# Nine landing buffers through the expert stage, experts taken in pairs, with table loads and projections placed elsewhere

## The reference: what is computed

```python
x = x + jnp.concatenate([fox_out, rwkv_out], axis=-1) @ w_out[i]   # fox_out has a factor sigmoid(fog)
x = x + moe_ffn(rmsnorm(x, moe_norm[i]), w_router[i], b_router[i], w_gu[i], b_gu[i],
                w_down[i], b_down[i])
gate = jax.nn.sigmoid(rmsnorm(x, ple_norm[i]) @ w_ple_gate[i])
x = x + gate * (p[i] @ w_ple_proj[i])
return rmsnorm(x, final_norm)
# an expert: hh = xb @ w_gu[e] + b_gu[e]; glu = min(hh[:, :FF], 7); lin = clip(hh[:, FF:], -7, 7)
#            y = (glu * sigmoid(1.702 * glu) * (lin + 1)) @ w_down[e] + b_down[e]
```

## Time and profile before

| | |
|---|---|
| time, median of 3 runs | 1285.59 us |
| time of the profiled execution | 1289.38 us |
| its span, first to last instruction | 1287.6 us |
| TensorE busy / weight loads | 1191.3 us (93%) / 522.4 us |
| VectorE, ScalarE busy | 307.5 us (24%), 181.1 us (14%) |
| DMA | 434.97 MB, mean 338 GB/s; 428 to 429 GB/s in most slices of the second half |
| chain that ended last | DMA 46%, PE 46%, DVE 4%, ACT 2% |
| granted TensorE clock, mean | 0.971 |

### The profile page before, as it was taken

How to read it: one execution, slowest core, us unless ns; L and a number is a source line. 1 busy time by engine, 2 the same in 40 slices (tenths; PEclk the granted TensorE clock), 3 DMA queues, 4 the chain that set the end, 5 groups by cost and what they waited for, 6 DMA issues and landing times.

```text
span 1287.6 us, 16763 instructions
## 1 busy us (share of the span) xinstructions
PE 1191.3 (93%) x6900; PEld 522.4 (41%) x6900; DVE 307.5 (24%) x631; ACT 181.1 (14%) x331; POOL 0.2 (0%) x4
## 2 busy tenths in 40 slices
PE   6999996899999999999999999999999999999994
PEld 5888765654333333333333323233333233223333
DVE  2444533333121212111111112111112111111136
ACT  2411422133000000000000000000100000000022
POOL 0000000000000000000000000000000000000000
PEclk9999996698999999999999999999999999999997
DMA  9631020165969999999999999999999999999940
GB/s 385 263 132 67 23 87 26 39 240 220 394 281 427 429 429 428 429 429 428 429 429 428 429 428 429 429 428 429 429 429 428 429 429 429 428 429 429 429 183 33
DMA packets 31793, 434.97 MB, mean 338 GB/s; under 512 B 3921, under 2 KB 4049, under 8 KB 5265
## 3 DMA queue, kind: packets, MB, share of 16 engines
q1 hardware_dynamic: 31760, 434.50, 80.3%
HBM read 433.44 MB, written 1.05 MB: 337 GB/s over the span
## 4 chain that ended last, share of the span: by engine, by line
DMA 46%; PE 46%; DVE 4%; ACT 2%; issue 1%; SPq 0%; DVEq 0%; ACTq 0%
DMA ring<-in_we 46%; PE PS L785 21%; PE PS L450 7%; PE PS L492 3%; PE PS L634 2%; PE PS L587 1%; PE PS L745 1%; PE PS L760 1%; PE PS L863 1%; DVE ring L1517 1%; PE PS L462 1%; PE PS L455 1%; PE PS L799 1%; PE PS L686 1%; PE PS L564 1%
## 5 line engine op out<-in xcount | busy, mean ns | idle before, releaser
L785 PE MATMUL PS<-ring,FV 128*64 128x512 f32 x3024 | 680.6, 597 | 42.6 <-DMA ring<-in_we 41.9
L785 PEld LDWEIGHTS PS<-ring,FV 128*64 128x64 f32 x3024 | 207.4, 137 | 483.1 <-issue 392.5
L450 PE MATMUL PS<-hT,ring 128*128 128x256 f32 x416 | 95.0, 387 | 0.8 <-ACT hT L917 0.8
L450 PEld LDWEIGHTS PS<-hT,ring 128*128 128x128 f32 x416 | 79.5, 193 | 13.1 <-ACT hT L917 1.2
L1387 DVE TENSOR_SCALAR rz<-con,lora 64x64 f32<-64x64 f32 x30 | 7.4, 246 | 303.6 <-PE PS L785 303.6
L1466 DVE TENSOR_SCALAR hT<-PS 128x512 f32<-128x512 f32 x32 | 22.1, 691 | 197.6 <-PE PS L785 197.6
L1144 DVE TENSOR_TENSOR FV<-PS,prm 128x512 f32<-128x512 f32 x32 | 22.1, 691 | 184.7 <-PE PS L752 184.7
L1071 ACT ACTIVATE FV<-PS 128x512 f32<-128x512 f32 x32 | 19.1, 597 | 310.1 <-PE PS L826 310.1
L745 PE MATMUL PS<-xq,rz 128*64 128x512 f32 x256 | 62.0, 605 | 0.0
L760 PE MATMUL PS<-B,rz 64*128 64x512 f32 x248 | 61.6, 615 | 0.0
L1069 ACT ACTIVATE hT<-hT 128x512 f32<-128x512 f32 x32 | 20.1, 630 | 267.0 <-DVE hT L1458 267.0
(11 more groups left out here) (255 smaller groups left out, 736.2 us busy)
## 6 DMA issues: line engine op xcount, KB each, us to landing
ring<-in_we SPq DMA_DIRECT2D x189, 2048.0 KB, 23.1
ring<-in_wz SPq DMA_DIRECT2D x7, 2048.0 KB, 21.6
B<-in_we SPq DMA_DIRECT2D x3, 2048.0 KB, 7.7
ring<-in_wo SPq DMA_DIRECT2D x2, 2048.0 KB, 7.9
ring<-in_wgate SPq DMA_DIRECT2D x2, 2048.0 KB, 24.3
con<-in_con SPq DMA_DIRECT2D x1, 1181.0 KB, 7.2
xq<-in_x SPq DMA_DIRECT2D x2, 512.0 KB, 4.6
ring<-in_wz SPq DMA_DIRECT2D x1, 1024.0 KB, 9.4
```

Source lines behind the costliest of these rows:

```text
L450: mm = pe.matmul(bank(n % 4, SEQ), w[:, k, at:at + P], hT[:, k, :], **flags)
L785: mm = pe.matmul(PS[64 * h:64 * h + 64, bank_, :], lhs(4 * (q % 2) + k), w[:, k, h, :], start=(first and k == 0), stop=(q % 2 == 1 and k = ...
```

## The change

1. **Landing buffers.** The three `extra` buffers are kept for the whole expert stage. Pieces 0 to 2 of every item land in `ring[0..2]`; pieces 3 to 5 land in `ring[3..5]` for even items and in `extra` for odd ones. SP issues pieces 3 to 5 of item i+1 behind pieces 0 to 2 of item i, when item i-1 has used its own pieces 3 to 5. Only at the end is the order 0 to 5 for the last item.
2. **Pairs.** All engines' places in the buffers must be known in the program, so TensorE's and SP's loops take two items in a turn: items 0 and 1, then 14 turns, then the last two items written out. The number of items is rounded up to an even one.
3. **Projection.** The second half of `w_ple_proj` lands in `LZ` and `lora` during item 1 (two transfers of 256 KB); its products (`project_late`) run in the last item and behind the last scatter, and stay in PSUM. In routing only the first halves are computed, and the ranks of the first token block stand ahead of them.
4. **Sigmoid of the attention gate.** Instead of four Sigmoids among the `z` steps: four copies, and one Tanh over all 1024 columns (step `fg`) behind `ffl`; sigmoid(x) = (1 + tanh(x/2)) / 2, with the half in the values `FV`.
5. **Table loads in routing.** The set with both Ln and Exp is loaded before `var`; the copy `T11` stands ahead of the second `rms`.
6. **Tail.** The gate is ScalarE's Sigmoid, so `L1516` and `L1517` go; two table loads are added; the last chunk has a PSUM bank of its own, so its product does not wait for the chunk before; the last scaling is split over both engines, and four stores of 256 KB replace one of 512 KB and two of 256 KB. Gate weights land in slots 3 and 4, free since item 30.

```diff
+        wgate = ring[:, 3:5, :]
+        gfin = ring[:, 5, 0:D]
+        wproj1 = LZ[:, :, :].rearrange("p a b -> p (a b)"), lora[:, 0:PW]
...
+            def place(q, odd):
+                return extra[q - 3] if odd and q >= 3 else ring[:, q, :]
...
+            for q in range(6):
                 sp.wait_ge(s_used, q + 1)
-                expert_piece(1, q)
+                sp.dma_start(place(q, q < 3), t["we"][1 if q < 3 else 2, q]).then_inc(landed(q, q < 3), 16)
+            sp.wait_ge(s_used, 7)
+            for k in range(2):
+                sp.dma_start(wproj1[k], t["wproj"][1, :, k * PW:(k + 1) * PW]).then_inc(s_ple1, 16)
...
+            def stage(i, odd, qs=range(6)):
+                e = [sp.value_load(EI[0:1, bass.ds(i + a, 1)], min_val=0, max_val=NE - 1) for a in range(1 + (len(qs) > 3))]
+                for q in qs:
+                    sp.wait_ge(s_used, 6 * i + (q - 5))
+                    sp.dma_start(place(q, odd == (q < 3)), t["we"][bass.ds(e[q // 3], 1), q, :, :].rearrange("a p n -> (a p) n"))\
+                        .then_inc(landed(q, odd == (q < 3)), 16)
+            with sp.Fori(0, pairs) as p:
+                stage(2 * p + 2, False)
+                stage(2 * p + 3, True)
+            stage(2 * last_pair, False, range(3))
+            stage(2 * last_pair + 1, True, range(3))
...
+            with pe.Fori(0, pairs) as p:
+                item(2 * p + 2, False)
+                item(2 * p + 3, True)
+            item(2 * last_pair, False)
+            last_item = 2 * last_pair + 1
+            item(last_item, True, last=True)
...
+                if last:
+                    pe.wait_ge(s_ple1, 32)
+                    project_late(0)
                 pe.wait_ge(s_eact, i + 1)
...
             scatter_last()
+            project_late(1)
...
-            pe.wait_ge(s_tact, tact_at["gate3"])
             finish(gates(1, 1, range(KD), 256, 512), "tpe", "gate4")
...
-                    fin(act.activation(FG[:, n - 22, :], bank(n % 4, SEQ), ACT.Sigmoid), f"z{n}")
+                    fin(act.activation(FG[:, n - 22, :], bank(n % 4, SEQ), ACT.Copy), f"z{n}")
...
+                        act.preload_act_table_set("exp_and_others")
+                        act.wait_ge(s_act, act_at[f"z{NZ - 1}"])
+                        fin(act.activation(FG[:, :, :], FG[:, :, :], ACT.Tanh, scale=0.5), "fg")
...
+            act.preload_act_table_set("natural_log_exp_and_others")
             pe_done("var")
...
+            turned(1, 1)
             rms(1)
-            turned(1, 1)
...
+            act.preload_act_table_set("sigmoid_and_others")
+            act.wait_ge(s_tact, tact_at["rstd1"])
+            gated(0, 0, 0, 512, 0, 0)
...
-                fin_t(v.tensor_scalar(sig, sig, 1.0, None, ALU.add), f"one{g}")
-                fin_t(v.reciprocal(sig, sig), f"inv{g}")
-                fin_t(tt(sig, PP[:, b, c0:c1], sig, ALU.mult), f"gp{g}")
+                v.wait_ge(s_tpe, tpe_at["pl1"])
+                fin_t(tt(sig, p, sig, ALU.mult), f"gp{g}")
                 fin_t(tt(xs[:, b, c0:c1], xs[:, b, c0:c1], sig, ALU.add), f"x4{g}")
```

More of the change, by code:

```diff
@@ L412, in _ @@
+            sp.wait_ge(s_tdve, tdve_at["out11"])
+            store(1, 1)
+            sp.wait_ge(s_tact, tact_at["out01"])
+            store(0, 1)
+            sp.wait_ge(s_tdve, tdve_at["out00"])
+            store(0, 0)
+            sp.wait_ge(s_out, 16 * 4)
         @block.tensor
@@ L770, in scatter_last, with product @@
                     finish(mm, "tpe", f"s{b}")
[L772 to L782 removed]
+            def product(i, odd, q, bank_, lhs, first):
+                weights = extra[q - 3] if odd and q >= 3 else ring[:, q, :]
+                w = weights.rearrange("p (k h c) -> p k h c", k=4, h=2)
+                if q < 3:
+                    pe.wait_ge(s_we[q], 16 * i + 16)
+                elif odd:
+                    pe.wait_ge(s_odd[q - 3], 8 * i + 8)
+                else:
+                    pe.wait_ge(s_we[q], 8 * i + 16)
                 for k in range(4):
@@ L792, in _, with item @@
             x_of, act_of = half_of(xT), half_of(aT)
-            def item(i, first=False, last=False):
+            def item(i, odd, first=False, last=False):
                 pe.wait_ge(s_ohb, i + 1)
@@ L1106, in _, with root @@
-            CHUNKS = ((0, 0, 512), (0, 512, 1024), (1, 0, 512), (1, 512, 768), (1, 768, 1024))
-            for g, (b, c0, c1) in enumerate(CHUNKS):
-                q = c0 // PW
+                    square(f"sq{b}{q}", 2 * b + q, xs[:, b, q * PW:(q + 1) * PW], PW * (2 * b + q))
+            def root(name, dst, ss, bias):
+                fin_t(act.activation(dst, ss, ACT.Ln, bias=bias, scale=1.0 / D), f"ln{name}")
+                act.wait_ge(s_tact, tact_at[f"ln{name}"])
+                fin_t(act.activation(dst, dst, ACT.Exp, scale=-0.5), f"rstd{name}")
@@ L1120, in _ @@
-            act.wait_ge(s_tdve, tdve_at["fin2"])
-            act.wait_ge(s_tact, tact_at["root1"])
-            fin_t(act.activation(xs[:, 1, 0:PW], xs[:, 1, 0:PW], ACT.Copy, scale=col[:, 15:16]), "out2")
+                square(f"sq{g}", 20 + g, xs[:, b, c0:c1], 4 * PW + (PW * g if g < 3 else 3 * PW))
+            transposed(0)
+            act.preload_act_table_set("natural_log_exp_and_others")
+            act.wait_ge(s_tdve, tdve_at["half0"])
+            act.wait_ge(s_tact, tact_at["sq01"])
@@ L1606 @@
             "brt": rep(a["b_router"]), "gfin": rep(a["final_norm"]),
-            "pT": chunks(a["p"][0, 0].T), "wproj": chunks(a["w_ple_proj"][0]),
+            "pT": chunks(a["p"][0, 0].T), "wproj": np.stack([chunks(a["w_ple_proj"][0][:, q * PW:(q + 1) * PW]) for q in range(2)]),
             "wo": np.stack([chunks(a["w_out"][0][:, q * PW:(q + 1) * PW]) for q in range(2)]),
```

243 lines of the change are left out of this document (122 added, 121 removed).

## The result

In one comparison the changed kernel took 1281.45 us (median of 6 runs, 1277.59 to 1284.25) and the kernel before 1288.03 us (6 runs, 1284.89 to 1289.76). The ratio is 0.9948, 95% interval 0.9925 to 0.9972: faster by 6.6 us, about half of the 13.5 us that were forecast, and 1.45 us above the forecast range. Two later comparisons gave the same: 7.2 and 7.9 us. The base matters too: the forecast took its gain off 1285.59 us, the median of the first 3 of those 6 runs; in the four comparisons the kernel before had medians of 1288.0, 1288.4, 1287.1 and 1285.7 us.

The account below looks back on a forecast made before the run. It took the expert stage to be bound by TensorE up to about 540 us, then by a full DMA queue. Terms +3.8 - 7.2 + 0.2 - 10.3 = -13.5 off 1285.6 gave 1272 us, range 1263 to 1280.

Parts of the forecast that it names:

- routing: Stage from `var` to item 0: earlier copies, ranks ahead of the projection and half its weights give -7.2 us, bounds -3.5 and -8.
- experts: Expert stage: the filled hole's 11.3 us lead is spent on the longer way behind the last wait, +0.2 us.
- tail: End of the kernel: gate products run without a stop and TensorE bounds the chunks, -10.3 us, bounds -7 and -12.
- mixing: Ahead of `q5`: table load and Tanh on the path +2.3, clock 1.5, sum +3.8 us, bounds +2.3 to +5.7.
- allowance of 1.5 us: Mixing: added for a possible fall to half clock after TensorE stands idle for 2.5 us.
- the lead counts in full: Rival: DMA alone decides the experts' end, so 11.3 us come on top, 1261 us; chance 0.08.
- the third term: Expert stage: the late half of the projection's weights delays the landing of item 30's piece 2 by 1.2 us.
- The work behind the last wait: Expert stage: TensorE's work from item 30's piece 2 to the stage's end, counted as 46.2 us.
- its four passes cost 1.7 at full clock: Routing: the halved first projection was to take 1.7 us once its weights landed at 295.8.
- one of the bounds (-3.5): Routing's smaller gain, if the clock stays at half through the ranks or the weights land as late as before.
- routing meets its transfer: Rival: projection weights land as before and the clock stays low, 3.7 us lost, 1276 us; chance 0.10.
- The jump: Rival: TensorE's doubled loop stalls at its jump back; at 8 us a turn 49 us, 1321 us; chance 0.06.

Follow-up runs that it names:

- E1: The changed kernel again with no edit, compared with the kernel before: median 1281.21 us, ratio 0.9928.
- E3: The changed kernel with the attention gate as before, four Sigmoids among the z steps and no Tanh: median 1277.16 us, ratio 0.9907 to the kernel before.
- E9: The kernel before with only mixing's edit, plain gate copies and one Tanh with its table load ahead of `q5`: median 1290.1 us, ratio 1.0034.
- E11: The changed kernel once more as it is, beside a run with mixing as before: 1277.77 us, ratio 0.9937 to the kernel before.
- E10: The changed kernel with the mixing stage as before, measured a second time: 1274.5 us, ratio 0.9911 to the kernel before.
- E2: The changed kernel with the weight stream back in the order 0 to 5 of each item from item 19 on: median 1265.53 us, ratio 0.9819.
- E5: The kernel before with only the nine buffers, paired loops and new order of the weight stream: median 1287.38 us, ratio 0.9996.
- E4: The changed kernel with the late half of the projection's weights issued ahead of the last item's pieces 0 to 2, not in item 1: median 1275.53 us, ratio 0.9906.
- E8: The changed kernel with natural stream order from item 19, the attention gate as before and late projection weights issued near the end: median 1264.31 us, ratio 0.9824.
- E6: The changed kernel with the tail's gate again as Exp, addition and reciprocal, the last chunk keeping its own bank: median 1286.70 us, ratio 1.0011.
- E7: The kernel before with only routing's table load moved ahead of `var` and `T11` copied ahead of the second `rms`: median 1287.00 us, ratio 0.9995.

## Why the prediction was half right

Measured terms: routing, experts and tail from the profiles (three executions of the kernel before's form of a stage, nine of the changed routing, six of the changed expert stage), mixing from the medians.

| term, us | forecast | measured | from |
|---|---|---|---|
| mixing | +3.8 | +3.9 | E1 less E3 4.05, E9 4.4, E11 less E10 3.3 |
| routing | -7.2 | -5.0 | 51.4, 51.9, 52.5 against 44.7 to 48.1, mean 46.9 |
| experts | +0.2 | +2.5 | 925.5 three times, against 927.3 to 928.7, mean 928.0 |
| tail | -10.3 | -9.6 | 52.2 to 52.3, against 42.6 |
| sum | -13.5 | -8.2 | medians: -6.6, -7.2, -7.9 |

**Mixing** was right, in its mechanism (the wait for `q5`, 2.56 us) and in its size. The allowance of 1.5 us for a clock that "need not happen" to fall was sound too: the clock fell right behind the wait in four of seven executions, at up to 1.6 us each (E9), about 0.9 in the mean. The remaining half microsecond can't be told from the spread: the granted clock later in this stage differs so much between executions of one program (mixing 258.3, 258.7 and 267.65 us) that no single pair tells.

**Experts.** The main claim held: the hole was filled, the last wait moved to piece 2 of item 30, the loop did not stall, and the lead was spent by three more pieces ahead of the last wait. E2 shows it, by giving 12.4 us of the stage back with nothing but another order; "the lead counts in full" falls for the changed kernel's order. The sizes of these two terms held as well: E5 has the new order and the filled hole but not the projection's transfers, and there the piece is used 3.7 us later than in before, where 14.7 - 11.3 = 3.4 was counted.

The step that failed is the third term, "the late half of the projection's weights, 0.5 MB at 428 GB/s, is in the stream (+1.2)". With these transfers the piece is used 879.8 to 881.3 us behind item 0's bias (six profiles), 1.9 to 3.3 later than in E5; without them, in E4, 0.6 later. The prediction counted the transfers by their bytes and not what SP does around them, the register loads of the next pieces, which now stand at a point where the queue runs dry: 1.3 us by E4, 1.5 by E8 against E2. I had asked of each moved transfer what it weighs and not what is issued behind it. How much of the term it is beyond these two values stays open, since the six profiles alone differ by 1.5 us. The work behind the last wait was 0.6 more than counted: 46.8 us to the end of the last expert product instead of 46.2.

**Routing.** By its steps the forecast held to 0.4 us where the clock stayed up: E4 took 44.65, 6.8 less than before. What failed is "its four passes cost 1.7 at full clock": in six of nine profiles the clock fell in this stage, and in E11 the first projection took 3.78 us for its run of four, at half clock, and the stage 47.75. The clock's fall was one of the bounds (-3.5); the value should have lain between, at -5. E7 adds that the terms of this stage don't add up one by one: taking away the first wait alone gave 0.1 us.

**Tail.** Right within 0.7 us, with TensorE as the bound. The split is E6's: 7.8 of it are the reciprocals.

**The sum.** Of the 6.3 us between forecast and the mean of three gains (7.2), 2.2 are routing's, most of it the clock, 2.3 the experts' and 0.7 the tail's; about 1 lies in the spread. The forecast time missed by a further 2.4 us, since its base, the first 3 runs, lay that much under the median of all 6. With an own range of 1266 to 1278 around a base known to no better than 2.5 us, the range was too narrow on the slow side. Of the other rivals, "routing meets its transfer" came in part: the wait for the projection's weights is 0.24 us in the first profile and up to 1.1 (E1), and the low clock that it names came in six profiles of nine. The jump cost nothing.

## What to carry to other kernels

Where an engine waits for a stream, a longer lead pays only if the last wait of all moves forward with it: follow one piece, the last that is waited for, and count how many pieces stand ahead of it in the old and the new order; here a change of order from item 19 on gave 12.4 us in its stage, where the whole change had gained 7.2. When a transfer is put into a program-ordered queue, look at what the issuing engine does next, not only at the bytes. And a wait that is taken away is gone only if the next thing behind it is ready; judge gains of a few microseconds by several executions of each kernel, stage by stage, since one pair of profiles showed 12.1 us where the medians show 7.2.

## What the runs showed of the hardware

- The same program at the same place ran its recurrence at a granted clock of 0.50, 0.68, 0.78 (230 to 262 us, three executions of the changed kernel), with spans of 1286.0, 1276.1 and 1275.5 us. Runs of one kernel spread by 14 us (1273.96 to 1287.85); nearly all of this in the profiled executions is in mixing and routing, while experts and tail repeat within 1.5 and 0.3 us.
- SP needed 2.5 us between two transfers when it read three values from memory into registers between them; the queue lost 1.2 us of its flow there.
- Behind a wait of 2.56 us in the recurrence the granted clock of the next 4.5 us was 0.62 to 0.65 in four executions and 1.00 in three; behind a wait of 0.18 us at the same place it was 1.00 in all six.
- A loop body of two items, some 520 TensorE instructions, jumps back with no gap; from 420 to 1190 us there was no instruction transfer at all.
